# Twelve low-part subtractions of one mixer on VectorE between the conditioning sums, and two loads earlier

## The chip, the cores and the metric

One Trainium2 chip; the kernel runs on one core. The metric is the device time of one execution in microseconds (us), the median over several runs.

## What is computed

Two transformer blocks over 512 tokens of width 1024, in float32. The change is in the first block. Cut to what matters:

```python
c_act = jax.nn.silu(c)
mod = (c_act @ ada_w + ada_b)                    # conditioning: 1024 -> 6 * 1024
sh_t, sc_t, g_t, sh_c, sc_c, g_c = jnp.split(mod, 6, axis=-1)
h = rms_norm(x, tm_pre_g) * (1.0 + sc_t) + sh_t
# token mixer ("mixer 1"): four branches y0..y3, four gates of 1024 columns each
gates = jax.nn.sigmoid(h @ w_gate + merge_gate_b)
merged = gates[0] * y_ml + gates[1] * y_gla + gates[2] * y_conf + gates[3] * y_sc
y = merged @ w_o
x = x + g_t * rms_norm(y, tm_post_g)             # then a convolutional FFN with sh_c, sc_c, g_c
```

The first third of the conditioning (`sh_t`, `sc_t`) is needed at once; the other two thirds (`g_t` and later) only after `w_o`.

## The kernel before, in words

**Precision and units.** Every large product is computed as three matmuls: each operand is split into a high part (a value rounded for TensorE, `w_hi`, `h_hi`) and a low part (the remainder, `w_lo`, `h_lo`), and hi*hi + hi*lo + lo*hi is summed in PSUM (lines 1207 to 1212: L1210, L1211, L1212). The weights stream through in units of 128x2048 floats (1 MB, two loads of 512 KB by the SP queue) and two buffers of each kind (`w_raw`, `w_hi`, `w_lo`). A unit gives TensorE 48 matmuls of 512 columns: two output tiles of 24 for a `gate` or `wo` unit, eight tiles of 6 for a branch unit `y0` to `y3`. A unit passes through four hands:

1. SP loads `w_raw` (L481). `before(u)` makes it wait until the low part of unit u-2 is made, since that frees `w_raw`.
2. ScalarE writes the high part, `split(u)` (L704 to L709). It waits for the load and for TensorE to have finished unit u-2 (`w_used`).
3. VectorE or GpSimd writes the low part, `lo(u)`: `w_raw - w_hi`, one tensor_tensor of 128x2048. L1735 is VectorE's, L625 GpSimd's. Which engine takes which unit is written out by hand. It waits only for the high part.
4. TensorE waits for the low part (`weights_ready`) and runs the unit.

**Unit numbers.** In the stretch around the change: 23 is `y2`, 24 to 27 are `gate0`, 28 is `y0`, 29 to 32 are `gate1`, 33 is `y1`, 34 to 37 are `wo`, 38 is the first of `up1`. In the kernel before GpSimd makes the low parts of all of 23 to 38 in one loop (L650 and L651).

**Order on TensorE** (L1513 on): `y2`; then the four `gate0` units, `y0`, the four `gate1` units, `y1`, the four `wo` units. After some of these units it runs `ada_columns` (L1221), matmuls of one column (L1229) that put the conditioning sums of two blocks across partitions. The tiles of PSUM go in turn over four banks, so the fifth tile of `y0` or `y1` needs the first one read by VectorE, and the first unit of `wo` starts on the banks of `y1`'s tiles four and five (counted from zero).

**Conditioning sums.** `ada_w` is read in 24 blocks of 128x2048 floats (1 MB). Blocks 8 to 23 are loaded during this stretch by ScalarE's DMA queue (L231), two after a unit as the table `ADA_LOADED` says, into four slots in turn; from block 12 on a load waits until TensorE has turned block n-4 in the same slot. `ada_sum(n)` (L1770) adds a block up on VectorE: one tensor_scalar of 128x256 (L1775) and seven scalar_tensor_tensor of 128x256 (L1777), each after the one before. The table `ADA_TURNED` says after which unit TensorE turns a block.

**Order on VectorE** (L2110 to L2123), written by hand and run in that order: `gated("y2")`, the low parts of the branch input, sums 8 to 13, `gated("y0")`, sums 14 to 21, `gated("y1", last=True)`, sums 22 and 23, then the gains. `gated` goes through eight tiles: product of PSUM tile and gate (L2013), which releases the bank; one tile later the addition to `merged` (L1994); with `last`, one more tile later `merged_low` (L1999), the low part of `wo`'s input, for which ScalarE first writes the high part (L954).

**Order on ScalarE** (L935 to L964): for every gate unit `split(u+1)` and then the sigmoid of its two tiles (L756), then `ada_more`, the loads of that place. After `y1` comes `merged_hi`, then `split` of unit 35.

Of the kernel before, what the change touches and what calls it, by code (L numbers as in the profile page):

```python
# [149 lines left out]
def program(nc, A, out):  # L150
# [10 lines left out]
    with ctx:  # L161
        def sb(name, shape, dt=FP32):
            return ctx.enter_context(nc.sbuf_tensor(name, shape, dt))
# [3 lines left out]
        def sem(name):  # L167
            if name not in sems:
                sems[name] = ctx.enter_context(nc.semaphore(name))
            return sems[name]  # L170
# [9 lines left out]
        y_lo = sb("y_lo", [P, 4, S], F32R)  # L180
# [45 lines left out]
        def ada_place(n):  # L226

            return ada_pairs[n % 4][:, :, n // 4 * 2 * P:(n // 4 + 1) * 2 * P] if n < 8 else ada_later[(n + 2) % 4]

        def ada_load(eng, n):  # L230
            eng.dma_start(ada_place(n), A["ada_w"][0][:, n * 2 * P:(n + 1) * 2 * P].rearrange("(k p) n -> p k n", p=P))\  # L231
               .then_inc(sem(f"ada_in{n % 8}"), 16)
# [5 lines left out]
        def vector_load(eng, g):  # L238
            r = 0
            for name, n in VECTORS[g]:  # L240
# [6 lines left out]
                else:  # L247
# [3 lines left out]

        ADA_LOADED = {(0, 0): (8, 9), (0, 1): (10, 11), (0, 2): (12, 13), (0, 4): (14, 15),
                      (1, 0): (16, 17), (1, 1): (18, 19), (1, 2): (20, 21), (1, 3): (22, 23)}
        ADA_TURNED = {(0, 2): (8, 9), (0, 3): (10, 11), (0, 4): (12, 13),
                      (1, 1): (14, 15), (1, 2): (16, 17), (1, 3): (18, 19), (1, 4): (20, 21)}
        ml_q, ml_k, ml_o = area(R, MT, S), area(R + 1024, MT, S), area(R + 2048, MT, S)
        ml_v = area(R + 3072, TT, MH * VW)
        ml_p, ml_h, ml_nm = area(R + 4128, 2, TT, S), area(R + 8224, TT, MIX), area(7232, S)  # L260
# [53 lines left out]
        def release(ins, t):  # L314
            ins.then_inc(read[t.bank], 1)
# [16 lines left out]
        U, unit = {}, 0  # L332
# [10 lines left out]
        def loaded_at(u):  # L343
            return 32 * (u // 2 + 1) + (16 if u >= IFA and (u - IFA) % 2 == 0 else 0)
# [263 lines left out]
        def _(pool):  # L608
# [38 lines left out]
                                       const("chunk_of").unsqueeze(2).broadcast_to([P, CPT, HD]), ALU.mult)\  # L647
                        .then_inc(sem("gl_placed"), 1)

            for u in range(U["y2"], U["up1"] + 1):  # L650
                lo(u)  # L651

            def hidden(n, conv_done):
# [45 lines left out]
        def _(act):  # L699
# [4 lines left out]
            def split(u, i=0, units=0):  # L704

                act.wait_ge(loaded[u % 2], loaded_at(u) + (i * 16 if units else 0))
                if u >= 2:
                    act.wait_ge(w_used, u - 1 + i)
                act.activation(w_hi[u % 2][:, :], raw[u % 2][:, :], ACT.Copy).then_inc(hi_done, 1)  # L709
# [48 lines left out]
            def gate_step(name, c, bias, u, used):  # L758

                split(u + 1)  # L760
                for k in range(2):
                    cc = 2 * c + k
                    if used is not None:
                        wait_read(act, T[used][cc])
                    out_of(T[name][cc], gates[:, cc, :], ACT.Sigmoid, **({} if bias is None else {"bias": col("merge_gate_b", bias + cc)}))
# [15 lines left out]
            u = U["sc"]  # L781
# [25 lines left out]
            u = U["ml"]  # L807
# [61 lines left out]
            u = U["gla"]  # L869
# [65 lines left out]
            def ada_more(b, c):  # L935

                for n in ADA_LOADED.get((b, c), ()):
                    if n == 8:
                        act.wait_ge(sem("y_lo"), 8)
                    if n >= 12:  # L940
                        act.wait_ge(sem("ada_turned"), n - 3)
                    ada_load(act, n)
# [260 lines left out]
        def _(pe):  # L1203
# [310 lines left out]
            for k in range(2):  # L1514
                for c in range(4):
                    column_unit(U[f"gate{k}"] + c, T[f"gate{k}"][2 * c:2 * c + 2])
                    for p in ADA_TURNED.get((k, c), ()):
                        ada_columns(T["ada1"][0], p, 8)
                branch_unit(f"y{k}", 2 * k, 6 + 2 * k)
                for p in ADA_TURNED[(k, 4)]:  # L1520
                    ada_columns(T["ada1"][0], p, 8)
# [207 lines left out]
        def _(dve):  # L1729
            ch = Chain(dve, "dve_step")  # L1730

            def lo(u, i=0):

                dve.wait_ge(hi_done, u + 1 + i)
                dve.tensor_tensor(w_lo[u % 2][:, :], raw[u % 2][:, :], w_hi[u % 2][:, :].bitcast(FP32), ALU.subtract)\  # L1735
                   .then_inc(parted[u % 2], 1)
# [33 lines left out]
            def ada_sum(n, unit):  # L1770

                dve.wait_ge(sem(f"ada_in{n % 8}"), 16 * (n // 8 + 1))
                if n < 4:
                    dve.wait_ge(sem(f"ada_in{n + 4}"), 16)
                ch.link(dve.tensor_scalar(unit[:, 0, :], unit[:, 0, :], c_act[:, 0:1], None, ALU.mult))  # L1775
                for k in range(1, KT):
                    ins = dve.scalar_tensor_tensor(out=unit[:, 0, :], in0=unit[:, k, :], scalar=c_act[:, k:k + 1], in1=unit[:, 0, :],  # L1777
                                                   op0=ALU.mult, op1=ALU.add)
                    if k < KT - 1:
                        ch.link(ins)  # L1780
                ins.then_inc(sem("ada_summed"), 1)
# [44 lines left out]
            u = U["sc"]  # L1826
# [171 lines left out]
                dve.wait_ge(sem("h_hi"), hn[0])  # L1998
                dve.tensor_tensor(h_lo[:, c, :], merged[:, c, :], h_hi[:, c, :].bitcast(FP32), ALU.subtract).then_inc(sem("h_ready"), 1)  # L1999

            def gated(name, bias=None, first=False, last=False):

                for c in range(KT):
                    t = T[name][c]
                    wait_full(dve, t)
                    if GATE_OF[name] in ("gate2", "gp", "ga") or name == "y3" and c < KT - 1:
                        dve.wait_ge(sem(f"{GATE_OF[name]}_open"), c + 1)
                    else:
                        wait_read(dve, T[GATE_OF[name]][c])
                    dst = merged[:, c, :] if first else product(c)  # L2010
                    if not first and gn[0] >= 2:
                        dve.wait_ge(sem("added"), gn[0] - 1)
                    ins = dve.scalar_tensor_tensor(out=dst, in0=bank[t.bank][:, :], scalar=0.0 if bias is None else col(bias, c),  # L2013
                                                   in1=gates[:, c, :], op0=ALU.add, op1=ALU.mult)
                    release(ins, t)

                    if not first and c:
                        add(T[name][c - 1], c - 1)
                    if last and c >= 2:
                        merged_low(c - 2)  # L2020
                if not first:
                    add(T[name][KT - 1], KT - 1)
                if last:
                    for c in (KT - 2, KT - 1):
                        merged_low(c)
# [55 lines left out]
            for c in range(MT):  # L2081
# [17 lines left out]
                for hh in range(2):  # L2099
                    n = 2 * c + hh  # L2100
# [6 lines left out]
                    release(dve.copy_predicated(gl_at[:, :, :], const("block_causal").bitcast(U32).unsqueeze(1).broadcast_to([P, TT, P]),  # L2107
                                                bank[t.bank][:, :].rearrange("p (a b) -> p a b", a=TT)), t)
            gla_norm(1)
            gated("y2", "conf_out_b")  # L2110
            for k in range(2):
                y_lo_of(gl_k[:, k, :], 2 + k, 7 + k)
            for n in range(8, 14):
                ada_sum(n, ada_place(n))
            gated("y0")
            for n in range(14, 22):
                ada_sum(n, ada_place(n))
            gated("y1", last=True)

            for n in (22, 23):  # L2120
                ada_sum(n, ada_place(n))
            ada_out(T["ada1"][0], 2 * KT, 4 * KT)
            wait_read(dve, T["ada1"][0])  # L2123
            ch.tick(dve.tensor_tensor(gain[:, 1, :], mod[:, 2 * KT:3 * KT], col("tm_post_g", 0, KT), ALU.mult))
# [341 lines left out]
            for c in range(4):  # L2466
                for k in range(2):
                    t = T["wo2"][2 * c + k]
                    wait_full(dve, t)
                    n = 2 * c + k  # L2470
# [59 lines left out]
```

## Time and profile before

| what | value |
|---|---|
| three runs, us | 1713.07, 1717.52, 1718.58 (median 1717.52) |
| the profiled execution's own time | 1712.64 us |
| its span, first to last instruction | 1710.5 us |
| mean granted TensorE clock | 0.972 |
| TensorE matmul busy | 1620.7 us (95%), 7536 matmuls |
| VectorE busy | 944.8 us (55%) |
| ScalarE busy | 608.4 us (36%) |
| GpSimd busy | 306.5 us (18%) |

In the profile PE is TensorE's matmuls, PEld its weight loads, DVE is VectorE, ACT is ScalarE, POOL is GpSimd, SP the sync engine; a trailing q names the engine's DMA queue. L1210 is line 1210 of the kernel. A row of a timeline has: start in us from the span's start, duration, engine, line, operation, output<-inputs, count, and in brackets the idle time of the engine ahead of it with what ended it. Runs of equal instructions are merged in one row with the time from the first start to the last end.

### The profile page before, as it was taken

Reading aid. Unit: us, or ns where it says so; the run is one execution under the profiler, and the core shown is the slowest. Engines: PE = TensorE matmul, PEld = TensorE weight load, DVE = VectorE, ACT = ScalarE, POOL = GpSimd, SP = SyncE. Lnnn points to the kernel's source line nnn. Section 1 sums busy time; section 2 is a strip of 40 time slices with the busy share of each in tenths; the row PEclk is TensorE's granted clock in tenths of the full one; section 3 lists DMA queues with packets and bytes.
Section 4 is the critical chain, followed back from the end, with each engine's and each line's share of the span. In section 5 each row is a group of like instructions: output and inputs, shape, how many; then the busy total and the mean of one; then the engine's idle time right before and its main releaser. Section 6 shows DMA issues by size and latency. Waiting matters only on the chain.

```text
span 1710.5 us, 19770 instructions
## 1 busy us (share of the span) xinstructions
PE 1620.7 (95%) x7536; PEld 1304.5 (76%) x7536; DVE 944.8 (55%) x1260; ACT 608.4 (36%) x758; POOL 306.5 (18%) x145
## 2 busy tenths in 40 slices
PE   5899999989899799999999899999999999999997
PEld 3687678768777588888888676877787888888886
DVE  5649455426987744444433657856334655556333
ACT  4243353232233433333322522344443433334222
POOL 1220024224343111111000000243353111111000
PEclk8899999989999899999999999999999999999999
DMA  9232212205582223333222124322122333332221
GB/s 333 69 98 83 66 61 88 75 25 179 190 270 82 67 74 98 98 98 98 99 98 98 50 84 122 87 75 75 50 84 88 95 92 97 98 98 98 100 96 49
DMA packets 192034, 170.42 MB, mean 100 GB/s; under 512 B 9511, under 2 KB 180868, under 8 KB 191972
## 3 DMA queue, kind: packets, MB, share of 16 engines
q1 hardware_dynamic: 174096, 150.16, 28.6%
q10 hardware_dynamic: 16948, 16.89, 3.1%
q0 software_dynamic: 928, 2.52, 0.4%
q8 instruction: 42, 0.69, 0.2%
q14 instruction: 20, 0.16, 0.0%
HBM read 165.54 MB, written 2.10 MB: 98 GB/s over the span
## 4 chain that ended last, share of the span: by engine, by line
PE 80%; DVE 12%; ACT 2%; issue 2%; DMA 2%; POOL 1%; SPq 1%; DVEq 0%; ACTq 0%
PE bank L1210 24%; PE bank L1212 23%; PE bank L1211 23%; DVE work L1777 5%; DMA work<-in_ada_w 2%; ACT w_hi L709 1%; PE bank L1217 1%; DVE work L1865 1%; DVE w_lo L1735 1%; PE bank L1218 1%; PE bank L1219 1%; PE bank L1674 1%; PE bank L1482 1%; PE bank L1302 1%; PE bank L1659 1%
## 5 line engine op out<-in xcount | busy, mean ns | idle before, releaser
L1210 PE MATMUL bank<-h_hi,w_hi 128*128 128x512 f32 x1536 | 614.9, 400 | 21.7 <-DVE h_lo L2228 5.0
L1211 PE MATMUL bank<-h_lo,w_hi 128*128 128x512 f32 x1536 | 604.1, 393 | 0.0
L1212 PE MATMUL bank<-h_hi,w_lo 128*128 128x512 f32 x1536 | 603.9, 393 | 0.0
L1210 PEld LDWEIGHTS bank<-h_hi,w_hi 128*128 128x128 f32 x1536 | 292.3, 190 | 105.5 <-issue 34.6
L709 ACT ACTIVATE w_hi<-w_raw 128x2048 fp32r<-128x2048 f32 x131 | 250.1, 1909 | 279.4 <-PE bank L1212 255.4
L1212 PEld LDWEIGHTS bank<-h_hi,w_lo 128*128 128x128 f32 x1536 | 292.0, 190 | 62.4
L1211 PEld LDWEIGHTS bank<-h_lo,w_hi 128*128 128x128 f32 x1536 | 292.6, 190 | 60.0 <-issue 1.0
L1735 DVE TENSOR_TENSOR w_lo<-w_raw,w_hi 128x2048 fp32r<-128x2048 f32 x88 | 202.6, 2302 | 244.6 <-ACT w_hi L709 244.2
L625 POOL TENSOR_TENSOR w_lo<-w_raw,w_hi 128x2048 fp32r<-128x2048 f32 x43 | 201.5, 4687 | 496.1 <-ACT w_hi L709 496.0
L1210 PE MATMUL bank<-y_hi,w_hi 128*128 128x512 f32 x480 | 191.3, 398 | 13.3 <-DVE tbuf L2013 8.4
L1212 PE MATMUL bank<-y_hi,w_lo 128*128 128x512 f32 x480 | 189.1, 394 | 0.0
L1211 PE MATMUL bank<-y_lo,w_hi 128*128 128x512 f32 x480 | 188.7, 393 | 0.0
L661 POOL TENSOR_TENSOR work<-work 128x512 f32 x44 | 57.2, 1299 | 457.8 <-ACT work L1019 457.8
L1210 PEld LDWEIGHTS bank<-y_hi,w_hi 128*128 128x128 f32 x480 | 91.5, 191 | 36.0 <-DVE tbuf L2013 9.2
L1777 DVE SCALAR_TENSOR_TENSOR work<-work,small 128x256 f32<-128x256 f32 (+1 forms) x140 | 113.7, 812 | 5.0
L1211 PEld LDWEIGHTS bank<-y_lo,w_hi 128*128 128x128 f32 x480 | 91.5, 191 | 19.2 <-issue 0.5
L1212 PEld LDWEIGHTS bank<-y_hi,w_lo 128*128 128x128 f32 x480 | 91.2, 190 | 19.5
L2197 DVE SCALAR_TENSOR_TENSOR work<-bank,par,work 128x511 f32<-128x511 f32 (+1 forms) x88 | 61.5, 743 | 77.8 <-ACT work L1013 77.8
L1013 ACT ACTIVATE work<-work,par 128x512 f32<-128x512 f32 x44 | 35.8, 815 | 106.7 <-DVE work L2186 106.7
L1013 ACT ACTIVATE work<-bank,par 128x512 f32<-128x512 f32 x44 | 30.0, 686 | 107.3 <-PE bank L1212 107.1
L2197 DVE SCALAR_TENSOR_TENSOR work<-work,par 128x511 f32<-128x511 f32 (+1 forms) x88 | 61.9, 746 | 9.6 <-ACT work L1013 9.6
L756 ACT ACTIVATE work<-bank,par 128x512 f32<-128x512 f32 x32 | 21.9, 686 | 119.0 <-PE bank L1212 119.0
(258 smaller groups left out, 1358.5 us busy)
## 6 DMA issues: line engine op xcount, KB each, us to landing
w_raw<-in_w_in SPq DMA_DIRECT2D x94, 512.0 KB, 4.7
w_raw<-in_ffn_w_up SPq DMA_DIRECT2D x44, 512.0 KB, 4.6
w_raw<-in_w_up SPq DMA_DIRECT2D x44, 512.0 KB, 4.9
work<-in_ada_w ACTq DMA_DIRECT2D x16, 1024.0 KB, 7.2
w_raw<-in_ffn_w_down SPq DMA_DIRECT2D x22, 512.0 KB, 3.9
w_raw<-in_w_down SPq DMA_DIRECT2D x22, 512.0 KB, 3.6
work<-in_ada_w SPq DMA_DIRECT2D x8, 1024.0 KB, 13.0
w_raw<-in_w_o SPq DMA_DIRECT2D x8, 512.0 KB, 4.0
```

The source lines that it names most:

```text
L625: pool.tensor_tensor(w_lo[u % 2][:, :], raw[u % 2][:, :], w_hi[u % 2][:, :].bitcast(FP32), ALU.subtract)\
L661: pool.tensor_tensor(work[:, bass.ds(i * (2 * S) + k * S, S)], cbuf[:, k, 0, :], cbuf[:, k, 1, :], ALU.mult).then_inc(sem("hid" + n), 1)
L709: act.activation(w_hi[u % 2][:, :], raw[u % 2][:, :], ACT.Copy).then_inc(hi_done, 1)
L756: release(act.activation(dst, src, func, **kw), t)
L1013: act.activation(cbuf[:, k, part, :], src, ACT.Identity, scale=par[:, bass.ds(i * 2 + at, 1)], **kw).then_inc(sem("center" + n), 1)
L1210: pe.matmul(dst, w_hi[s][:, at:at + n], hi, start=first, stop=False)
L1211: pe.matmul(dst, w_hi[s][:, at:at + n], lo, start=False, stop=False)
L1212: return pe.matmul(dst, w_lo[s][:, at:at + n], hi, start=False, stop=last)
L1217: pe.matmul(dst, hi, w_hi[s][:, at:at + n], start=first, stop=False)
L1735: dve.tensor_tensor(w_lo[u % 2][:, :], raw[u % 2][:, :], w_hi[u % 2][:, :].bitcast(FP32), ALU.subtract)\
L1777: ins = dve.scalar_tensor_tensor(out=unit[:, 0, :], in0=unit[:, k, :], scalar=c_act[:, k:k + 1], in1=unit[:, 0, :], op0=ALU.mult, op1=ALU.add)
L2197: ins = dve.scalar_tensor_tensor(out=c[:, back:S], in0=src[:, 0:S - back], scalar=w, in1=c[:, back:S], op0=ALU.mult, op1=ALU.add)
```

## The change

It does four things. (1) GpSimd makes the low parts of units 23 and 36 to 38 alone; the twelve units 24 to 35 move to VectorE, in its order: one after the fourth product of each of `y2`, `y0`, `y1` (units 24, 29, 34), the others ahead of a pair of sums or ahead of a branch. (2) The sums are cut into pairs: 8 to 13 stay ahead of `y0` and 14 to 21 ahead of `y1`, each pair behind one low part. (3) Blocks 8 and 9 are loaded within the first gate unit, before ScalarE's reads of its tiles; the loads behind them move up by up to one place. (4) TensorE turns most blocks one place earlier, and blocks 12 and 13 before `y0` instead of behind it.

```diff
-        ADA_LOADED = {(0, 0): (8, 9), (0, 1): (10, 11), (0, 2): (12, 13), (0, 4): (14, 15),
-                      (1, 0): (16, 17), (1, 1): (18, 19), (1, 2): (20, 21), (1, 3): (22, 23)}
-        ADA_TURNED = {(0, 2): (8, 9), (0, 3): (10, 11), (0, 4): (12, 13),
-                      (1, 1): (14, 15), (1, 2): (16, 17), (1, 3): (18, 19), (1, 4): (20, 21)}
+        ADA_LOADED = {(0, 0): (10, 11), (0, 1): (12, 13), (0, 2): (14, 15), (0, 3): (16, 17),
+                      (1, 0): (18,), (1, 1): (19, 20), (1, 2): (21, 22), (1, 3): (23,)}
+        ADA_TURNED = {(0, 1): (8, 9), (0, 2): (10, 11), (0, 3): (12, 13), (0, 4): (),
+                      (1, 0): (14,), (1, 1): (15, 16), (1, 2): (17, 18), (1, 3): (19, 20), (1, 4): (21,)}
...
-            for u in range(U["y2"], U["up1"] + 1):
+            lo(U["y2"])
+            for u in range(U["wo"] + 2, U["up1"] + 1):
                 lo(u)
...
             def gate_step(name, c, bias, u, used):
                 split(u + 1)
+                if u == U["gate0"]:
+                    act.wait_ge(sem("y_lo"), 8)
+                    for n in (8, 9):
+                        ada_load(act, n)
...
                 for n in ADA_LOADED.get((b, c), ()):
-                    if n == 8:
-                        act.wait_ge(sem("y_lo"), 8)
...
-            def gated(name, bias=None, first=False, last=False):
+            def gated(name, bias=None, first=False, last=False, low_at=None):
...
                     release(ins, t)
+                    if low_at and c == 3:
+                        lo(low_at)
...
-            gated("y2", "conf_out_b")
+            gated("y2", "conf_out_b", low_at=U["gate0"])
             for k in range(2):
                 y_lo_of(gl_k[:, k, :], 2 + k, 7 + k)
-            for n in range(8, 14):
-                ada_sum(n, ada_place(n))
-            gated("y0")
-            for n in range(14, 22):
-                ada_sum(n, ada_place(n))
-            gated("y1", last=True)
-
-            for n in (22, 23):
-                ada_sum(n, ada_place(n))
+            lo(U["gate0"] + 1)
+            sums(8, 9)
+            lo(U["gate0"] + 2)
+            sums(10, 11)
+            lo(U["gate0"] + 3)
+            sums(12, 13)
+            lo(U["y0"])
+            gated("y0", low_at=U["gate1"])
+            lo(U["gate1"] + 1)
+            sums(14, 15)
+            lo(U["gate1"] + 2)
+            sums(16, 17)
+            lo(U["gate1"] + 3)
+            sums(18, 19)
+            lo(U["y1"])
+            sums(20, 21)
+            gated("y1", last=True, low_at=U["wo"])
+
+            lo(U["wo"] + 1)
+            sums(22, 23)
```

`sums(a, b)` calls `ada_sum(n, ada_place(n))` for each of its numbers.

## Rows read from the trace of the kernel before

**Rows 1.** The page, part 4: the chain that ended last, share by engine.
```profile
PE 80%; DVE 12%; ACT 2%; issue 2%; DMA 2%; POOL 1%; SPq 1%; DVEq 0%; ACTq 0%
```

**Rows 2.** Who waited for whom, PE, 375 to 560 us: total, times, longest.
```profile
PE bank L1210 <- DVE tbuf L2013: 8.4, 2, 4.5
```

**Rows 3.** Timeline of PE, 450 to 535 us.
```profile
450.67 0.50 PE L1210 MATMUL bank<-y_hi,w_hi 128*128 128x512 f32 x1 [4.52 <-DVE tbuf L2013]
...
457.85 0.95 PE L1229 MATMUL bank<-small,work 128*128 128x1 f32 x8
...
514.61 0.50 PE L1210 MATMUL bank<-y_hi,w_hi 128*128 128x512 f32 x1 [3.87 <-DVE tbuf L2013]
...
533.43 0.39 PE L1212 MATMUL bank<-h_hi,w_lo 128*128 128x512 f32 x1
534.38 0.50 PE L1210 MATMUL bank<-h_hi,w_hi 128*128 128x512 f32 x1 [0.56 <-POOL w_lo L625]
```

**Rows 4.** Windows, PE alone: us, busy (count), granted clock, DMA share, GB/s.
```profile
450.70:454.40 3.70, 3.70 (x10) 0.56 0.25 84
...
514.70:518.30 3.60, 3.60 (x11) 0.68 0.66 228
```

**Rows 5.** Timeline of DVE, 385 to 605 us.
```profile
387.81 3.17 DVE L1994 TENSOR_TENSOR work<-work,tbuf 128x512 f32<-128x512 f32 x1
...
399.07 1.28 DVE L1760 TENSOR_TENSOR y_lo<-work,y_hi 128x512 fp32r<-128x512 f32 x2
413.08 1.10 DVE L1775 TENSOR_SCALAR work<-work,small 128x256 f32<-128x256 f32 x1 [12.74 <-DMA work<-in_ada_w]
414.22 3.61 DVE L1777 SCALAR_TENSOR_TENSOR work<-work,small 128x256 f32<-128x256 f32 x7
...
418.13 7.84 DVE L1777 SCALAR_TENSOR_TENSOR work<-work,small 128x256 f32<-128x256 f32 x7
...
475.23 2.58 DVE L1775 TENSOR_SCALAR work<-work,small 128x256 f32<-128x256 f32 x1 [3.21 <-DMA work<-in_ada_w]
...
513.88 1.28 DVE L2013 SCALAR_TENSOR_TENSOR tbuf<-bank,work 128x512 f32<-128x512 f32 x2
...
527.09 1.48 DVE L1999 TENSOR_TENSOR h_lo<-work,h_hi 128x512 fp32r<-128x512 f32 x2
...
582.68 2.28 DVE L1735 TENSOR_TENSOR w_lo<-w_raw,w_hi 128x2048 fp32r<-128x2048 f32 x1
```

**Rows 6.** Timeline of POOL, 330 to 605 us.
```profile
420.28 4.88 POOL L625 TENSOR_TENSOR w_lo<-w_raw,w_hi 128x2048 fp32r<-128x2048 f32 x1 [6.25 <-ACT w_hi L709]
```

**Rows 7.** Lines of DVE, shapes apart: count | busy us, mean ns | idle before.
```profile
L1777 DVE SCALAR_TENSOR_TENSOR work<-work,small 128x256 f32<-128x256 f32 x112 | 92.6, 827 | 4.0
```

**Rows 8.** Timeline of ACT and its DMA queue, 405 to 605 us.
```profile
406.27 0.69 ACT L756 ACTIVATE work<-bank,par 128x512 f32<-128x512 f32 x1 [3.47 <-PE bank L1212]
406.30 1.04 ACTq L231 DMA_DIRECT2D work<-in_ada_w  x2
...
417.15 0.69 ACT L756 ACTIVATE work<-bank,par 128x512 f32<-128x512 f32 x1 [4.75 <-PE bank L1212]
...
428.04 0.69 ACT L756 ACTIVATE work<-bank,par 128x512 f32<-128x512 f32 x1 [4.76 <-PE bank L1212]
...
439.87 0.69 ACT L756 ACTIVATE work<-bank,par 128x512 f32<-128x512 f32 x1 [4.76 <-PE bank L1212]
...
469.95 1.01 ACTq L231 DMA_DIRECT2D work<-in_ada_w  x2
...
527.75 1.90 ACT L709 ACTIVATE w_hi<-w_raw 128x2048 fp32r<-128x2048 f32 x1
```

**Rows 9.** The page, part 6: DMA issues, KB each, median us to landing.
```profile
w_raw<-in_w_in SPq DMA_DIRECT2D x94, 512.0 KB, 4.7
...
work<-in_ada_w ACTq DMA_DIRECT2D x16, 1024.0 KB, 7.2
work<-in_ada_w SPq DMA_DIRECT2D x8, 1024.0 KB, 13.0
```

More of the change, by code:

```diff
@@ L2109, in _, with sums @@
             gla_norm(1)
-            gated("y2", "conf_out_b")
+            gated("y2", "conf_out_b", low_at=U["gate0"])
             for k in range(2):
                 y_lo_of(gl_k[:, k, :], 2 + k, 7 + k)
-            for n in range(8, 14):
-                ada_sum(n, ada_place(n))
-            gated("y0")
-            for n in range(14, 22):
-                ada_sum(n, ada_place(n))
-            gated("y1", last=True)
-            for n in (22, 23):
-                ada_sum(n, ada_place(n))
+            def sums(*parts):
+                for n in parts:
+                    ada_sum(n, ada_place(n))
+            lo(U["gate0"] + 1)
[17 more added lines that the diff above has]
+            sums(22, 23)
             ada_out(T["ada1"][0], 2 * KT, 4 * KT)
```

## The prediction

> **What bounds the kernel now.** I read the page's chain first: most of it is TensorE [rows 1], so a change pays only where it lets TensorE run without a gap or at its full clock. Next I asked who made TensorE wait in the stretch the diff touches (375 to 560 us). The reader is to see one releaser that matters: VectorE's product of branch and gate, twice [rows 2]. The timeline places both waits: 4.52 us in the middle of `y0` and 3.87 us in the middle of `y1`; a third, 0.56 us, is for GpSimd's low part of unit 35 [rows 3]. Behind each of the long waits the granted clock is down, 0.56 and 0.68 as the mean of a short stretch [rows 4], so part of it runs at 1.2 instead of 2.4 GHz.
>
> Last I asked why VectorE is late. It waits once for its first block, 12.74 us [rows 5], and from then on works through conditioning sums without a gap until `y0`. The seven chained instructions of a sum take 3.61 us in one case and 7.84 us in the next [rows 5], and the long one lies on a low part of GpSimd, 420.28 to 425.16 [rows 6]. Over all 16 sums of the stretch the mean instruction takes 827 ns [rows 7] against 3.61 / 7 = 516, so 112 x 0.311 = 34.8 us are lost, the excess of eight long sums. A GpSimd low part that meets a sum costs VectorE 7.84 - 3.61 = 4.2 us, nearly twice what it takes on VectorE itself, 2.28 us [rows 5].
>
> The Trainium skill, "SBUF — State Buffer", section "Who interferes with whom", gives the reason: a VectorE instruction with two SBUF inputs and a GpSimd instruction that reads SBUF exclude each other, and the second waits for all of the first. The rows agree, with 4.2 us lost to a low part of 4.88.
>
> **Terms I use.** A unit is 417.15 - 406.27 = 10.88 us of TensorE; one followed by the columns of two blocks is 439.87 - 428.04 = 11.83 us [rows 8], so turning two blocks costs 0.95 us and one about 0.47. A tile of a branch is an eighth, 1.36 us. A unit's matmuls end about 0.3 us before the read that marks it. A sum alone on its engines is one start to the next, 418.13 - 414.22 = 3.91 us, a pair 7.8 [rows 5]. A low part on VectorE is 2.28 us. Product, addition and `merged_low` are about 0.6 us each; `gated("y1")` as a whole takes from 513.88 to 528.57, 14.7 us, or 1.84 per tile [rows 5].
>
> **Part 1, the first gate units.** The low part of unit 24 sits behind the fourth product of `y2`, about 390.6 to 392.9; TensorE wants it at 395.1. It delays the later products of `y2` by 2.3 us, but one addition that took 3.17 us beside GpSimd, instead of some 0.6, runs free, so the branch's low parts end at 400.35 as before [rows 5]. Unit 25: 400.4 to 402.6, wanted at 406.0. ScalarE issues loads 8 and 9 at 400.4 instead of 406.30, 5.9 earlier. What queues behind its new wait is the sigmoid of a tile whose bank is wanted again four tiles later: cost nothing. How long load 8 takes is not shown for this place. The nearest rows are 469.95 to 475.23, 5.3 us, and 406.30 to 413.08, 6.8 us [rows 5, 8]; the median is 7.2, and that of the eight loads at the kernel's start 13.0 [rows 9]. I take 6.8, since a weight load lies beside it as there; 13.0 is kept for the range. Sums 8 and 9 run 407.2 to 415.0, the low part of 26 to 417.3. TensorE ends unit 25 at 416.9, turns two blocks and wants unit 26 at 417.8. This is the tightest place: 0.5 us.
>
> **Part 2, the pace.** From here VectorE needs 7.8 + 2.3 = 10.1 us per unit against TensorE's 11.83, and gains 1.7 each time. Low part against wanted: unit 27 at 427.4 against 429.7; unit 28 at 437.5 against 441.5. VectorE is then free before the first tile of `y0` is full at 442.9. **The wait of 4.52 us and its slow clock are gone.** Products follow TensorE at 1.36 per tile; the low part of 29 lies behind the fourth, to 449.9, wanted at 452.4; the fifth product, at about 451.1, still frees the bank before `gate1`. `gate1` starts at 452.4; in the profile before it starts at 457.85 + 0.81 = 458.7 [rows 3], with the same columns behind it. Gain here 6.3 us.
>
> **Part 3, gate1 and y1.** Low parts, limited now by ScalarE's high part as well: unit 30 at 457.7 (wanted 463.7), 31 at 469.1 (475.6), 32 at 480.9 (487.4), 33 at 492.7 (499.2). Sums 20 and 21 end at 500.5 and the first tile of `y1` is full at 500.6. **The wait of 3.87 us and its slow clock go too.** `gated("y1")` with the low part of 34 inside takes 14.7 + 2.3 and some waits for tiles, to about 518.1. TensorE ends `y1` at 510.1, turns one block, and starts `wo` at 510.6 with a wait of 0.3 for a bank. From there it needs 10.9 us, to 521.8; the eighth low part at 518.1 is early enough. ScalarE's high part of unit 35 then lies at 517.6 to 519.5 (before 527.75 to 529.65 [rows 8]), VectorE's low part at 519.6 to 521.9. The second `wo` unit starts at 522.0 instead of 534.38.
>
> **What moves along.** SP's loads wait for the low parts of two units before, so each shifts with them; they need 4.7 us [rows 9] and have at least 10, also beside a pair of conditioning loads. GpSimd keeps 36 to 38 at the same distance from TensorE. Sums 22 and 23 start at 521.9 and are wanted two units later. Behind `wo` nothing changes, and all of it shifts. If one of these covers failed, the price would be that of rival A.
>
> **The sum.** 534.38 - 522.0 = 12.4 us. Seen from the other side: removed are 4.52 + 3.87 and the gap 533.66 to 534.38, 0.7; from 450.67 to 457.85 TensorE runs 24 matmuls, half a unit or 5.44 us, in 7.18; from 514.61 to 533.66 it runs 72 and the columns of two blocks, 16.32 + 0.95, in 19.05; that is 1.7 + 1.8 more [rows 3]. Together 12.6, less the bank wait of 0.3. Against the profiled execution, 1712.64, that is 1700.2. The median of the runs shown is 4.9 us above it; on that base it is 1705.1, and I take 1705.
>
> **Rivals.**
>
> A, late once. A load lands late or a low part misses its unit. Were load 8 to take 13.0 us, the low part of 26 would be 6.2 - 0.5 = 5.7 us late, and the slow clock behind such a wait costs 1.75 (from rows 3). Gain 12.4 - 7.4 = 5.0, so 1712.5. For it: only 0.5 us of slack there. Against: those 13.0 us come from the kernel's start with eight such loads. Several misses of a microsecond would give the same. 0.14.
>
> B, nothing gained. VectorE pays for low parts what it gains on sums, so that both waits stay. That needs blocking to cost VectorE only 2.3 us per low part; then the time is 1717.5. For it: eight of sixteen sums are not long, so some low parts of GpSimd cost VectorE little. Against: the lost 34.8 us alone are more than 12 x 2.28 = 27.4, and the four low parts ahead of `y0` give up 9.1 us where three long sums lose 12.7. 0.07. The Trainium skill's "Perfetto Trace Analysis", section "Optimizing Scalar/DVE Operations", warns of this: since the two share a port, moving operations between them might not help. Here it would leave the sum at zero.
>
> C, slower. The sums stay long with GpSimd idle, because something else stretches them (the loads written beside them). The point is 11.83 - 2.28 = 9.55 us per pair: below it VectorE keeps up, above it TensorE waits at every unit. Alternating pairs of 12.0 us, as now, would add nine low parts, 20.5 us, ahead of `y1`'s first product, less 5.9 for the earlier load and 3.2 for the wait before block 16 [rows 5]. That is 11.4 later, with one low part more and a shorter one for unit 35 cancelling out: 1728.9. Against it: the sum at 414.22 is short, 3.61 us, with the second of the two loads issued at 406.30 just landing behind it [rows 5, 8]. 0.05.
>
> The forecast has 0.74. On its own it spans 1700 to 1709, for the base and about 2 us of small waits. The range goes from 1697 to 1712, almost to rival A. About 0.3%, 5 us, is what a measurement of this kernel can tell from no change; A at 5 us counts as faster. Faster 0.88, same 0.07, slower 0.05.
>
> **What would show it.** Right: no wait of TensorE for L2013 over 1 us between 395 and 525; granted clock near 1.00 in both branch units; all sums at 3.6 us for seven; sum 8 starting near 407; `gate1` at 452.4 and the second `wo` unit at 522. Wrong: TensorE waiting for L1735 at unit 26 and behind (A), sums of 6 us or more without GpSimd beside them (C), or `gate1` still starting behind 457 (B).

## The result and the profile after

The changed kernel took 1700.61 us in the median of four runs (1699.12 to 1701.09), the kernel before 1716.17 (1713.07 to 1718.58). The ratio is 0.9905, 95% interval 0.9893 to 0.9918: faster by 0.95%, about 15.6 us. One execution each of the kernel before, of the low parts back on GpSimd and of the loads in their old place took 2711, 3254 and 3872 us and is left out of the ratios below. The profiled execution of the changed kernel took 1700.69 us with a span of 1698.9, against 1712.64 and 1710.5: 12.0 us less.

First the view that answers to [rows 2], who made TensorE wait from 375 to 560 us in the changed kernel (total, times, longest). Lines behind the edits are three higher than before: L2016 is the product that was L2013, L1213 the matmul that was L1210.

```profile
PE bank L1503 <- ACT work L924: 1.2, 1, 1.2
PE bank L1325 <- issue: 0.7, 1, 0.7
PE bank L1213 <- DVE rstd L2016: 0.4, 1, 0.4
```

The two waits for VectorE, 8.4 us together, are gone; so is the one for GpSimd's low part. What is left of the kind is 0.4 us. (The wait of L1325 is not new: the kernel before has it at 569 us, outside the window.) The page's parts 1 and 4 show the same from above: GpSimd 57.8 us less busy than before, VectorE 11.9 us less although it makes twelve more low parts (1272 instructions instead of 1260), and in the chain that ended last VectorE at 8% where it was 12% [rows 1].

```profile
PE 1617.4 (95%) x7536; PEld 1302.0 (77%) x7536; DVE 932.9 (55%) x1272; ACT 608.6 (36%) x758; POOL 248.7 (15%) x133
...
PE 86%; DVE 8%; ACT 2%; issue 2%; DMA 1%; SPq 0%; POOL 0%; DVEq 0%; ACTq 0%
```

Why VectorE has less to do stands in its lines with the shapes kept apart. The row that answers to [rows 7] has the same 112 instructions at 485 ns each instead of 827.

```profile
L1780 DVE SCALAR_TENSOR_TENSOR work<-work,small 128x256 f32<-128x256 f32 x112 | 54.3, 485 | 4.0
```

The difference is 38.3 us, given back for twelve low parts of 2.29, 27.5 us. VectorE's timeline shows the order of the first gate units, answering to [rows 5]:

```profile
402.24 2.29 DVE L1738 TENSOR_TENSOR w_lo<-w_raw,w_hi 128x2048 fp32r<-128x2048 f32 x1
407.69 0.35 DVE L1778 TENSOR_SCALAR work<-work,small 128x256 f32<-128x256 f32 x1 [3.16 <-DMA work<-in_ada_w]
408.08 3.61 DVE L1780 SCALAR_TENSOR_TENSOR work<-work,small 128x256 f32<-128x256 f32 x7
411.98 0.35 DVE L1778 TENSOR_SCALAR work<-work,small 128x256 f32<-128x256 f32 x1 [0.28 <-DMA work<-in_ada_w]
412.37 3.61 DVE L1780 SCALAR_TENSOR_TENSOR work<-work,small 128x256 f32<-128x256 f32 x7
415.89 2.29 DVE L1738 TENSOR_TENSOR w_lo<-w_raw,w_hi 128x2048 fp32r<-128x2048 f32 x1
...
445.07 0.69 DVE L2016 SCALAR_TENSOR_TENSOR tbuf<-bank,work 128x512 f32<-128x512 f32 x1 [6.85 <-PE bank L1215]
...
521.75 2.29 DVE L1738 TENSOR_TENSOR w_lo<-w_raw,w_hi 128x2048 fp32r<-128x2048 f32 x1 [1.11 <-ACT w_hi L710]
```

In all sums the seven chained instructions take 3.61 us. One sum is still held, by the low part of unit 36 on GpSimd, but in its first instruction, which has one tensor input: 4.70 us where it takes 0.35 alone. Nothing waited for it.

```profile
527.87 4.70 DVE L1778 TENSOR_SCALAR work<-work,small 128x256 f32<-128x256 f32 x1
```

```profile
527.69 4.73 POOL L625 TENSOR_TENSOR w_lo<-w_raw,w_hi 128x2048 fp32r<-128x2048 f32 x1 [168.81 <-ACT w_hi L710]
```

At 445.07 VectorE waits 6.85 us for TensorE; before, TensorE waited for it. And the clock, by windows over the two stretches in which the waits lay (columns: us, busy and count of PE, PEld, DVE, ACT, POOL, then granted clock, DMA share, GB/s), here in the changed kernel:

```profile
445.00:465.00 20.00, 20.00 (x90) 16.55 (x89) 18.78 (x28) 3.76 (x3) 0.00 (x0) 1.00 0.65 205
510.00:530.00 20.00, 19.56 (x89) 15.88 (x88) 18.54 (x28) 9.60 (x13) 2.31 (x1) 1.00 0.32 106
```

The same two windows of the kernel before:

```profile
445.00:465.00 20.00, 15.48 (x66) 12.41 (x65) 19.62 (x24) 2.43 (x2) 6.74 (x2) 0.91 0.31 98
510.00:530.00 20.00, 16.14 (x68) 12.95 (x67) 19.72 (x31) 6.87 (x9) 2.90 (x2) 0.91 0.27 90
```

From 0.91 to 1.00 in both.

### The profile page after: what moved, and what is told of

It reads as the page before. It is cut to its first block, busy times and chain, and to the rows that moved or that the text cites. A ratio compares the mean times of both kernels' runs of the same rounds, so it can differ in the third digit from the quotient of the medians.

```text
span 1698.9 us, 19770 instructions
## 1 busy us (share of the span) xinstructions
PE 1617.4 (95%) x7536; PEld 1302.0 (77%) x7536; DVE 932.9 (55%) x1272; ACT 608.6 (36%) x758; POOL 248.7 (15%) x133
## 4 chain that ended last, share of the span: by engine, by line
PE 86%; DVE 8%; ACT 2%; issue 2%; DMA 1%; SPq 0%; POOL 0%; DVEq 0%; ACTq 0%
PE bank L1213 26%; PE bank L1215 25%; PE bank L1214 25%; DVE work L1780 1%; DVE w_lo L1738 1%; DMA work<-in_ada_w 1%; PE bank L1220 1%; DVE work L1868 1%; PE bank L1221 1%; PE bank L1222 1%; PE bank L1677 1%; ACT w_hi L710 1%; PE bank L1485 1%; PE bank L1305 1%; PE bank L1662 1%
## 5 line engine op out<-in xcount | busy, mean ns | idle before, releaser
L1213 PE MATMUL bank<-h_hi,w_hi 128*128 128x512 f32 x1536 | 614.8, 400 | 21.5 <-DVE h_lo L2249 5.0
L1213 PEld LDWEIGHTS bank<-h_hi,w_hi 128*128 128x128 f32 x1536 | 292.0, 190 | 105.6 <-issue 34.6
L1738 DVE TENSOR_TENSOR w_lo<-w_raw,w_hi 128x2048 fp32r<-128x2048 f32 x100 | 230.0, 2300 | 248.7 <-ACT w_hi L710 248.3
L625 POOL TENSOR_TENSOR w_lo<-w_raw,w_hi 128x2048 fp32r<-128x2048 f32 x31 | 143.7, 4635 | 542.8 <-ACT w_hi L710 542.7
L1213 PE MATMUL bank<-y_hi,w_hi 128*128 128x512 f32 x480 | 190.5, 397 | 4.9 <-DVE work L2016 3.6
L1213 PEld LDWEIGHTS bank<-y_hi,w_hi 128*128 128x128 f32 x480 | 91.0, 190 | 26.8 <-DVE work L2016 4.0
L1780 DVE SCALAR_TENSOR_TENSOR work<-work,small 128x256 f32<-128x256 f32 (+1 forms) x140 | 75.4, 538 | 5.0
```

What stands on the lines that cost most here:

```text
L625: pool.tensor_tensor(w_lo[u % 2][:, :], raw[u % 2][:, :], w_hi[u % 2][:, :].bitcast(FP32), ALU.subtract)\
L1213: pe.matmul(dst, w_hi[s][:, at:at + n], hi, start=first, stop=False)
```

## The experiments

Three questions were open. Is the gain the 12 us of the two profiles, or the 15.6 of the medians? Which part of the change makes it, the place of the low parts or the earlier loads? And is it GpSimd's reading that holds VectorE? All runs below were timed beside the kernel before on their chip.

### The changed kernel again

No edit.

> The changed kernel unchanged, beside the kernel before on one chip. The profile accounts for 12 us between the first tile of y2 and the second wo unit, the medians for 15.6. Theory 1: the mechanism is worth 12 us (ratio 0.993) and the rest was the spread of the kernel before over runs (1713 to 1718.6). Theory 2: the whole 15 us is the change (ratio 0.9905 to 0.991), and then some part of it lies where the two profiles don't show it.

Measured: 1700.99 us (1697.29 to 1702.97) against 1717.1, ratio 0.9906 (0.9891 to 0.9922). The larger number is real: 16.1 us. In the profile the stretch from the first product of `y2` to the second `wo` unit is short again. Theory 2 holds as far as the size goes; where the rest lies, two more profiles of the kernel before were to tell.

### Two more profiles of the kernel before

> The kernel before, for its profile alone: 15 of 20 of its executions beside the last runs took 1715.6 to 1718 us at a granted clock of 0.969 to 0.970, while the profiled one took 1712.6 at 0.972. Theory 1: a usual execution has longer stretches at the lower clock behind the two waits in y0 and y1 than the profiled one, which the change removes too (that closes the gap between 12 us in the profiles and 16 in the runs). Theory 2: the extra low clock lies elsewhere and has nothing to do with the waits.

> The same once more, since one execution can be either kind: about 1717 us at 0.969, with the time against the profile of before found between 445 and 535 us by theory 1.

Measured: 1719.36 and 1718.47 us, granted clock 0.967 and 0.969, one execution each. The two windows in the first of them:

```profile
445.00:465.00 20.00, 15.45 (x66) 12.47 (x65) 18.66 (x28) 3.16 (x3) 4.72 (x1) 0.83 0.55 175
510.00:530.00 20.00, 16.14 (x68) 13.04 (x67) 19.61 (x30) 7.05 (x8) 4.77 (x1) 0.83 0.56 181
```

The waits are as long as before, but the clock behind them is lower, 0.83 where the first profile had 0.91. TensorE's timeline of that profile shows it in matmuls:

```profile
456.01 0.79 PE L1210 MATMUL bank<-y_hi,w_hi 128*128 128x512 f32 x1 [4.55 <-DVE tbuf L2013]
...
464.07 0.95 PE L1229 MATMUL bank<-small,work 128*128 128x1 f32 x8
```

The 24 matmuls after the wait take 8.06 us, in the profile that the prediction read 7.18 [rows 3], at full clock 5.44. So the slow stretch behind one wait costs 2.6 us here, not 1.74. The second new profile has 8.16, and behind the wait in `y1` the two have 8.12 and 8.13 where the first had 7.23. That is 1.8 us more for both waits.

The whole stretch grows by half of that only. From the first matmul of `gate0` to the last columns of the sums (L1229, L1232 in the changed kernel) the three profiles of the kernel before take 161.2, 162.1 and 162.2 us, the two of the changed kernel 148.8 and 148.9. TensorE, held longer behind `y1`, comes later to unit 35 and no longer waits for its low part, which gives 0.9 us back. So what the change removes in its own stretch is 12.4 us of the profile that the prediction read and 13.3 us of the other two.

The larger difference between the profiles lies where the streams are alike. The two new spans are 6.7 and 5.0 us longer than the first, and 5.9 and 4.1 us of that have passed when `y2` begins: its first product came at 385.4, 391.3 and 389.5 us in the kernel before, and at 387.3 to 389.6 in the ten profiles of the changed kernel and its variants. It goes with the clock granted from 200 to 300 us, here in the profile that the prediction read and in the first new one (PE alone, columns as in [rows 4]):

```profile
200.00:300.00 100.00, 95.55 (x485) 0.98 0.24 74
```

```profile
200.00:300.00 100.00, 95.56 (x476) 0.93 0.24 74
```

Of all thirteen profiles the six that begin `y2` by 387.7 have 0.98 there, the six at 388.7 to 389.6 have 0.95, and the one at 391.3 has 0.93. So of what the new profiles have more than the first, Theory 1's slow clock in the stretch is 0.9 us and most of the rest is Theory 2's, a clock that was lower elsewhere. Why it differs there is open. The variants of the changed kernel show the same spread there, so it does not explain the gain of the medians: 13.3 of the 16 us lie in the stretch, and the other 2 to 3 are placed by no profile.

### The low parts back on GpSimd, the loads early

```diff
+            for u in range(U["y2"], U["up1"] + 1):
-            lo(U["y2"])
-            for u in range(U["wo"] + 2, U["up1"] + 1):
                 lo(u)
...
-                    if low_at and c == 3:
-                        lo(low_at)
...
-            lo(U["gate0"] + 1)
-            sums(8, 9)
...
+            sums(8, 9, 10, 11, 12, 13)
```

> The changed kernel with all twelve low parts back on GpSimd; the earlier loads and the earlier turns of the blocks stay. Theory A (the 4.2 us that VectorE loses to a low part of GpSimd are what made it late): sums are long again (7.8 us for seven in about every second one), the waits in y0 and y1 are back in part, and most of the gain is lost: 1708 us or more. Theory B (the earlier loads, 5.9 us for block 8 and 3.2 for block 16, would have been enough): sums long again, but VectorE reaches y0 near 443 to 445 and y1 near 503, before the fifth tile wants its bank, so both waits stay away; lost is only the later low part of unit 35, 2 to 4 us: 1703 to 1705 us.

Measured: 1711.44 us, ratio 0.9975 (0.9961 to 0.9988). By the ratio the loads alone give 4.3 us of the 16 (5.7 by the medians). The time is Theory A's, the timeline is half Theory B's. Who made TensorE wait:

```profile
PE bank L1212 <- DVE tbuf L2015: 2.5, 1, 2.5
PE bank L1231 <- DVE work L1779: 2.4, 2, 1.4
PE bank L1212 <- POOL w_lo L625: 2.0, 1, 2.0
```

The 2.4 us are new: with the blocks turned earlier, TensorE waits for the sums that it is to turn. The wait in `y0` is gone: VectorE stood ready there for 2.19 us, as B had it. The one in `y1` is not all gone, because VectorE came to it at 514.26 and not at 503. This execution came to `y2` 3.9 us later than the one B counted from; 7.3 us remain. B had counted the long sums only. VectorE's timeline shows what it left out:

```profile
442.64 3.61 DVE L1779 SCALAR_TENSOR_TENSOR work<-work,small 128x256 f32<-128x256 f32 x7
448.44 0.69 DVE L2015 SCALAR_TENSOR_TENSOR tbuf<-bank,work 128x512 f32<-128x512 f32 x1 [2.19 <-PE bank L1214]
449.82 0.69 DVE L2015 SCALAR_TENSOR_TENSOR tbuf<-bank,work 128x512 f32<-128x512 f32 x1 [0.69 <-PE bank L1214]
450.43 4.14 DVE L1996 TENSOR_TENSOR work<-work,tbuf 128x512 f32<-128x512 f32 x1
...
461.09 5.10 DVE L1996 TENSOR_TENSOR work<-work,tbuf 128x512 f32<-128x512 f32 x2
```

```profile
449.42 4.61 POOL L625 TENSOR_TENSOR w_lo<-w_raw,w_hi 128x2048 fp32r<-128x2048 f32 x1 [7.36 <-ACT w_hi L709]
```

Where no sum is there to be held, an addition of 0.68 us is, for 4.14, and two of 1.29 together take 5.10: 7.3 us lost. The product at 449.82, which takes one input from a bank of PSUM, lies beside the same low part and is not held. GpSimd's low parts cost VectorE most of their time wherever they meet an instruction with two inputs from SBUF.

### The loads in their old place, the low parts on VectorE

The tables `ADA_LOADED` and `ADA_TURNED` of the kernel before, and no early load in `gate_step`.

> The changed kernel with the loads of blocks 8 to 23 and the turns of the blocks in their old places; the twelve low parts stay on VectorE. Theory A (low parts on VectorE between sums do it alone): within 2 us of the changed kernel, since VectorE gains 1.7 us per unit. Theory B (the order on VectorE ties the low part of unit 26 to the landing of blocks 8 and 9, so the earlier load is a condition of the move): sum 8 starts near 413, the low part of 26 ends near 423, TensorE waits about 5 us for it ahead of unit 26 and runs a stretch at the lower clock behind it, 6 to 8 us more than the changed kernel, 1706 to 1709.

Measured: 1713.54 us, ratio 0.9979 (0.9970 to 0.9989). This half alone gives 3.6 us. Theory B was right about the tie but counted one wait where there are two. TensorE's timeline:

```profile
424.04 0.80 PE L1211 MATMUL bank<-h_hi,w_hi 128*128 128x512 f32 x1 [4.92 <-DVE w_lo L1736]
...
454.59 0.77 PE L1211 MATMUL bank<-y_hi,w_hi 128*128 128x512 f32 x1 [4.19 <-issue]
```

and VectorE's, with what it waited for:

```profile
413.88 0.35 DVE L1776 TENSOR_SCALAR work<-work,small 128x256 f32<-128x256 f32 x1 [9.32 <-DMA work<-in_ada_w]
...
421.70 2.28 DVE L1736 TENSOR_TENSOR w_lo<-w_raw,w_hi 128x2048 fp32r<-128x2048 f32 x1
...
444.38 0.35 DVE L1776 TENSOR_SCALAR work<-work,small 128x256 f32<-128x256 f32 x1 [9.67 <-DMA work<-in_ada_w]
...
452.20 2.28 DVE L1736 TENSOR_TENSOR w_lo<-w_raw,w_hi 128x2048 fp32r<-128x2048 f32 x1
```

The second is for the low part of unit 28, 452.20 to 454.48, though the profile calls it issue. The low part of unit 26 ends at 424.0, where the expectation had it near 423, and again at unit 28 a low part stands behind a sum whose block is not there: block 12's load goes out at 438.16, after TensorE has turned block 8 at 437.62. Alone the halves give 4.3 and 3.6 us, together 16.1: neither is the change without the other. Low parts between sums are only in time if the sums never wait, and early loads give little while GpSimd holds VectorE. The places of the loads and of the turns were changed together here, so no run tells them apart.

### Only the first pair early

The tables of the kernel before but for blocks 8 and 9, which are loaded early as in the change.

> The changed kernel with blocks 8 and 9 loaded early as there, but all later loads and all turns of blocks in their old places. The run with all loads in their old place showed two waits of TensorE, 4.9 us ahead of unit 26 and 4.2 ahead of y0. Theory 1: they are two separate causes, the landing of block 8 and, for block 12, the turn of block 8 on TensorE that frees its slot. Then the first wait is gone here and the second is there: block 12's load goes out only after TensorE has turned block 8 behind unit 26, near 431, and lands near 438, where VectorE would want it at 428; y0 waits 3 to 5 us. Time 4 to 8 us above the changed kernel. Theory 2: the second wait was only what the first left behind; then both are gone and the time is that of the changed kernel within 2 us.

Measured: 1709.05 us, ratio 0.9965 (0.9952 to 0.9978), 8 us above the changed kernel. Rows of TensorE, of VectorE and of ScalarE's DMA queue:

```profile
435.28 0.80 PE L1213 MATMUL bank<-h_hi,w_hi 128*128 128x512 f32 x1 [5.53 <-DVE w_lo L1738]
```

```profile
425.12 0.35 DVE L1778 TENSOR_SCALAR work<-work,small 128x256 f32<-128x256 f32 x1 [8.03 <-DMA work<-in_ada_w]
...
435.14 0.35 DVE L1778 TENSOR_SCALAR work<-work,small 128x256 f32<-128x256 f32 x1
```

```profile
429.34 1.01 ACTq L231 DMA_DIRECT2D work<-in_ada_w  x2
```

The wait ahead of unit 26 is gone, and one wait remains, so both theories miss. It is not where Theory 1 had it: the load of blocks 10 and 11 in its old place holds the low part of unit 27, 5.5 us. Block 12, issued at 429.34, is in time, because VectorE, itself held by block 10, comes to it only at 435.14. So it is not enough to move the first pair's load, the second pair's must move too. Whether the later ones must is not shown: from this wait on everything runs late enough for them.

### The low parts of the first two wo units back on GpSimd

```diff
-            for u in range(U["wo"] + 2, U["up1"] + 1):
+            for u in range(U["wo"], U["up1"] + 1):
...
-            gated("y1", last=True, low_at=U["wo"])
+            gated("y1", last=True)
...
-            lo(U["wo"] + 1)
```

> The changed kernel with the low parts of the first two wo units (34 and 35) back on GpSimd. Expected by the timeline: unit 35's low part takes 4.6 instead of 2.3 us behind a high part that ends at the same time, so TensorE waits about 2 us ahead of the second wo unit; the low part of 34 blocks VectorE once within the last branch, up to 4.6 instead of the 2.3 it takes there. 2 to 4 us slower than the changed kernel. Rival: hidden, within 1 us, since the eighth step of the first wo unit is what TensorE waits for in any case.

Measured: 1704.83 us, ratio 0.9936 (0.9915 to 0.9956), 3.8 us above the changed kernel; the intervals of the two just overlap. The six executions fall in two groups, 1700.1 to 1702.7 us at a granted clock of 0.978 and 1707.0 to 1709.2 at 0.973, and the profile is one of the first, so the cost in time is less sure than its cause. The row of TensorE is the one expected, a wait of 2.05 us for GpSimd:

```profile
527.50 0.50 PE L1213 MATMUL bank<-h_hi,w_hi 128*128 128x512 f32 x1 [2.05 <-POOL w_lo L625]
```

The other cost is there too: the low part of unit 34 (503.75 to 508.36) holds an addition of the last branch for 3.69 us instead of 0.68.

### GpSimd busy beside the sums, reading or only writing

```diff
             lo(U["y2"])
+            idle_out = area(R + 8192, 1536)
+            pool.wait_ge(sem("y_lo"), 8)
+            for n, u in enumerate([U["gate0"] + k for k in (2, 3, 4)] + [U["gate1"] + k for k in (1, 2, 3, 4)]):
...
+                pool.wait_ge(hi_done, u + 1)
+                pool.tensor_tensor(idle_out, cst[:, 0:1536], cst[:, 0:1536], ALU.subtract).then_inc(sem("beside"), 1)
```

In the second kernel the last line is `pool.memset(idle_out, 0.0)`. ScalarE waits for the seventh of them ahead of `merged_hi`, long after it is done.

> The changed kernel with seven more instructions on GpSimd, one at the time of each high part of units 26 to 28 and 30 to 33: a subtraction of 128x1536 that reads the constants and writes an unused area, about 3.5 us each. Nothing waits for them. By the forecast's own rule VectorE's round (two sums and a low part) grows from 10.1 to 13.5 us, over TensorE's 11.83: the low part of 26 is late by about 2 us, those of 27 and 28 by 1.7 more each; in gate1 the slack of 5 to 7 us takes most of it. 4 to 10 us slower than the changed kernel, with sums of about 7 us in the trace. If VectorE was not slowed by GpSimd's reading but by the low parts as such, no change.

> The same seven places on GpSimd with a memset of 128x1536, which reads nothing. If it is reading that shuts VectorE out, all sums stay at 3.6 us for seven and the time is that of the changed kernel within 1.5 us. If any work of GpSimd on the memory does, sums grow by its length as in the run before.

Measured: reading 1706.61 us, ratio 0.9941 (0.9923 to 0.9958); writing 1699.07, ratio 0.9909 (0.9883 to 0.9935). The reading kernel is 7.5 us slower than the writing one (5.5 by the ratios) and 5.6 us slower than the changed kernel, and no result of the reading is used. VectorE and GpSimd in the kernel that reads:

```profile
421.28 6.12 DVE L1788 SCALAR_TENSOR_TENSOR work<-work,small 128x256 f32<-128x256 f32 x7
```

```profile
423.34 2.75 POOL L657 TENSOR_TENSOR work<-cst 128x1536 f32<-128x1536 f32 x1 [8.35 <-ACT w_hi L717]
```

and in the one that writes:

```profile
423.70 1.44 DVE L1786 TENSOR_SCALAR work<-work,small 128x256 f32<-128x256 f32 x1
...
435.20 3.61 DVE L1788 SCALAR_TENSOR_TENSOR work<-work,small 128x256 f32<-128x256 f32 x7
...
469.25 2.29 DVE L1746 TENSOR_TENSOR w_lo<-w_raw,w_hi 128x2048 fp32r<-128x2048 f32 x1 [0.17 <-ACT w_hi L717]
```

```profile
423.61 1.38 POOL L657 MEMSET work<- 128x1536 f32 x1 [9.73 <-ACT w_hi L717]
...
435.45 1.38 POOL L657 MEMSET work<- 128x1536 f32 x1 [10.46 <-ACT w_hi L717]
...
469.34 1.38 POOL L657 MEMSET work<- 128x1536 f32 x1 [10.25 <-ACT w_hi L717]
```

A read of 2.75 us adds 2.5 us to a sum. A memset inside the seven instructions (435.45, in the sum at 435.20) adds nothing, nor does one inside VectorE's low part (469.34, in the one at 469.25); five of the seven memsets fall on instructions with two inputs, and none is held. The other two fall on the tensor_scalar of a sum, which has one, and do hold it. So for instructions with two inputs it is the reading that shuts VectorE out.

The expected rule holds in its direction. With 12.5 us for two sums, one of them long, and a low part, VectorE falls behind TensorE's 11.83, and unit 26, unit 27 and `y0` each wait 0.5 to 0.6 us. The expectation had them late by 2 us and then 1.7 more each; the instruction is shorter than it took, 2.75 instead of 3.5 us. In `gate1` no unit waits for its low part, but TensorE waits four times, 2.6 us in all, for the sums that it is to turn, which the expectation had not seen.

### The same in the second mixer

The changed kernel has one more wait of TensorE for GpSimd, at 1287 us, ahead of the second `wo2` unit:

```profile
1287.24 0.80 PE L1213 MATMUL bank<-h_hi,w_hi 128*128 128x512 f32 x1 [3.39 <-POOL w_lo L625]
```

```diff
-            for u in range(U["wo2"] + 1, U["up2"] + 1):
+            for u in range(U["wo2"] + 2, U["up2"] + 1):
...
+            lo(U["wo2"] + 1)
             for c in range(4):
                 for k in range(2):
                     t = T["wo2"][2 * c + k]
```

> The lesson carried to the second mixer: in the changed kernel TensorE waits 3.39 us near 1287 us for GpSimd's low part of the second wo2 unit, with the clock down behind it. Here that one low part (2.3 us instead of 4.6) is made by VectorE, idle at that time, ahead of the first residual addition. Expected: the wait shrinks to about 1.1 us, and the slow stretch behind it may go (up to 2.7 us): 2 to 5 us faster than the changed kernel. Rival: VectorE's later release of the first wo2 banks holds TensorE instead, no gain.

The second kernel has this too, and takes the first `wo2` unit's low part from GpSimd:

```diff
-                lo(U[after] + 2)
+                if name == "gp":
+                    lo(U[after] + 2)
...
                 opened("ya", c, product(c))
+                if c == 3:
+                    lo(U["wo2"])
...
             merged_hi(3)
-            log_and_exp()
...
                 split(U["wo2"] + c + 1)
+                if c == 0:
+                    log_and_exp()
```

> As the run before, and the low part of the first wo2 unit on VectorE too, behind the fourth product of ya (it held one of VectorE's subtractions for 4.68 us on GpSimd), and ScalarE's table load behind the high part of the second unit instead of ahead of it (1.28 us). Expected: no wait of TensorE ahead of the second wo2 unit; 4 to 7 us faster than the changed kernel, 1694 to 1697 us. Rival: TensorE's first wo2 unit follows VectorE's subtractions, which now hold a low part of 2.3 us in their midst, and nothing more than in the run before is gained.

Measured: 1696.11 us, ratio 0.9888 (0.9874 to 0.9902), and 1694.44 us, ratio 0.9881 (0.9867 to 0.9895). In the first the wait shrinks as expected:

```profile
1284.97 0.50 PE L1213 MATMUL bank<-h_hi,w_hi 128*128 128x512 f32 x1 [1.10 <-DVE w_lo L1738]
```

In the second there is none. Against the changed kernel's 1700.99 that is 4.9 and 6.5 us by the medians, but 3.1 and 4.3 by the ratios to the kernel before on the same chip, and the intervals of the ratios overlap the changed kernel's a little. The single times speak for a gain: the second kernel's lie between 1693.1 and 1696.0, all ten of the changed kernel between 1697.3 and 1703.0. The wait that goes is the firmer evidence. That the second beats the first is within their intervals.

## Why the prediction was right, and where its sizes were off

**The bound and the waits.** Right: both waits of TensorE for L2013 and their slow clock are gone, nothing came in their place, and the seven chained instructions are short in all sums.

**The schedule.** In the changed profile the stretch begins 1.88 us later than in the one before (first product of `y2` at 387.26 instead of 385.38). Less that offset, the forecast and the trace stand like this:

| step | forecast | profile after, less 1.88 |
|---|---|---|
| sum 8 starts | 407.2 | 405.8 |
| low part of unit 26 ends | 417.3 | 416.3 |
| first product of `y0` | 442.9 | 443.2 |
| first product of `y1` | 500.6 | 500.9 |
| low part of unit 35 | 519.6 to 521.9 | 519.9 to 522.2 |
| second `wo` unit starts | 522.0 | 522.3 |

Load 8 took 5.3 us, the lower of the two rows of before; 6.8 was taken. That had no effect: the slack at unit 26 was 1.6 us (418.18 to 419.75) instead of 0.5. The low part of unit 35, on the other hand, ends only 0.2 us before TensorE takes the unit up. The wait for a bank was 0.44 us, 0.3 forecast.

**The sum.** Forecast 12.4 us against the profiled execution, and the stretch itself, `gate0` to the last columns, gave 161.2 - 148.8 = 12.4; the two profiled executions as a whole differ by 12.0. Between the medians it was 15.6 to 16.1. The term that was mis-sized is the slow clock behind the two waits: 1.7 + 1.8 from one execution, while two more profiles of the same kernel showed 2.6 to 2.7 behind each. Half of that comes back at unit 35, so against those two profiles the stretch is worth 13.3 us, 0.9 more than forecast. The rest of the 3 to 4 us lies outside what the forecast summed, and no run gives its cause.

The time, 1705 forecast and 1700.61 measured, is inside the range. The forecast's own base, the profile's 1712.64, had given 1700.2, and that this is so near is luck: the base lay 3.5 us below the median and the gain 3.2 us short, and the two errors cancel.

**Blocked time.** "The excess of eight long sums" was one short, and so seven, not eight, of the sixteen are not long. The alone-time of an instruction was put at 3.61 / 7 = 516 ns, which holds the gaps too; the mean after is 485, so 38.3 us were lost, nine sums.

**Rival A.** Its mechanism is real: with the loads where they were, the low part of unit 26 makes TensorE wait 4.92 us, near the 5.4 that the forecast's own numbers give (406.3 + 6.8 + 7.8 + 2.3 against 417.8). It didn't come about because the loads moved with the low parts; load 8 took 5.3 us, far from A's 13.0. **Rival B** is out: sums were held 4.2 us by a low part that takes 2.3. The Trainium skill's warning ("Perfetto Trace Analysis", "Optimizing Scalar/DVE Operations") is that moving operations between the two might not help. In this case, from GpSimd to VectorE, it helped. **Rival C** did not happen, but its rule was tested by the seven reads: with 12.5 us per round instead of 10.1, TensorE waited for the low part at each of units 26 to 28, though not in `gate1`, where the slack was larger.

## What to carry to other kernels

GpSimd work that reads SBUF is not free for VectorE: while it runs, VectorE's instructions with two inputs from SBUF stand still (4.2 us lost to a low part of 4.6 to 4.9, 2.5 to a read of 2.75). So count nearly all of a GpSimd instruction's time on VectorE wherever the two meet, and if VectorE does the same work in less than it loses, give it the work. A conversion put in line behind sums is only as early as the loads of those sums: move the loads, and what frees their slots, in the same change. And take the clock behind a wait from several executions; here one profile was off by 0.9 us per wait.

## What the runs showed of the hardware that was not expected

A GpSimd memset, which reads nothing, left VectorE's instructions with two inputs alone (3.61 us for seven with the memset inside them) but held its tensor_scalar with one input: 1.44 us instead of 0.35 beside a memset of 1.38. In the changed kernel the same instruction takes 4.70 us beside a low part on GpSimd of 4.73. The Trainium skill, "SBUF — State Buffer", section "Who interferes with whom", has both halves: instructions with two inputs in SBUF meet GpSimd's reads only, while tensor_scalar can enter a mode that takes the port pair shared with GpSimd. The rows agree.

The same wait of 4.5 us is followed by a slow stretch of quite different length: 24 matmuls took 7.18 us in one execution and 8.06 and 8.16 in two others. The kernel that doesn't wait has no such stretch in either branch unit.
